# ScalarE evacuates the transposes before the exponential in every attention slot of a hybrid decoder layer

## The chip, the cores and the metric

The kernel runs on 1 core of one Trainium2 chip. The metric is device time in microseconds (us). An execution of the kernel before was also profiled: it took 1846.08 us, of which the program's instructions span 1844.3 us. The engines are called PE (TensorE), DVE (VectorE), ACT (ScalarE), POOL (GpSimd) and SP (SyncE).

## The reference

One decoder layer for 1024 tokens of width 1024. A normalised input is projected and mixed by three kinds of attention, whose outputs are gated per channel and projected; a grouped mixture of experts follows. Only the attention is touched here. Each query tile n (128 tokens, 8 tiles) does, cut to what matters:

```python
# NSA, 8 heads of 64, one KV head: compressed keys, selected blocks, window of 512
p_cmp = masked_softmax(q @ k_cmp, ...);  o_cmp = p_cmp @ v_cmp
_, sel = lax.top_k(block_scores(p_cmp), 8)
p = masked_softmax(q @ k_slc[sel], ...);  o_slc = p @ v_slc
p = masked_softmax(q @ k_win[last 512 + own tile], ...);  o_win = p @ v_win
# stick breaking, 4 heads: z = q @ k;  a = exp(z + running sum of -softplus(z));  o = a @ v
# sliding window of 128 with sinks, 4 heads
p = exp(s - max);  o = (p @ v) / (sum(p) + exp(sink - max))
```

A merge gate, `sigmoid(h @ w_in[merge columns])`, weights the three branches. Its matrix products do not depend on the attention.

## The kernel before

The attention is written as a list of slots. A query tile n from 0 to 7 has 20 slots, i from 0 to 19: `win` heads 0 to 7 at i = 0 to 7, then `slc` heads with a `swa` (sliding window) head at i = 9, 12, 15 and 18. Slot q = 20 n + i. Every slot has one unit (kind, head, n), with scores over `nb` blocks of 128 keys: n + 1 for `slc`, at most 5 for `win`, 2 for `swa` (1 at n = 0). A stick-breaking head (`sb`, n + 1 blocks) rides along in slots i = 6, 9, 12, 15.

In slot q, **PE** does in this order: the scores of unit q; the transposes of the units in `s["T"]`; the products with the values of units transposed earlier; the scores of the ride; and a third of a merge-gate product (8 matmuls of 512 columns; slots 2 to 147, but for two slots). `s["T"]` holds first the unit of slot q - 1. In 55 of 160 slots it holds a second one:

- i = 3: the compressed probabilities (`cmp`, 4 blocks)
- i = 4: the token outputs of tile n - 1 (`out`, 8 blocks; not at n = 0)
- i = 5: the selection mask (`sel`, 1 block)
- i = 10, 13, 16, 19: the `sb` unit of slot q - 4

Where there are two, the gate product is issued between the transposes of the first and those of the second (`if j == 1: gate_matmuls(q)`, L1985 to L1987). The values of the first unit follow the second's transposes, except with `sel` and `out`, where they come before them and nothing follows.

Transposes are written to PSUM in groups of up to 4 blocks. Groups have a running number g over all slots; even ones are evacuated by **ACT** (L396), odd ones by **DVE** (L398), both in `evacuate_groups`, which waits for `t_full` of each group. From the planner's numbering, the second unit has an even group in these slots: every `sb` (i = 10, 13, 16, 19 at every n), every `out`, `cmp` only for n of 4 and more, `sel` only for n below 4.

**DVE** in slot q: the row maximum of the scores of unit q (L1393, for `swa` L1389 and L1391, gives `max_ok`), its groups, softmax sums and other small work.

**ACT** in slot q, strictly in program order: waits for `max_ok`, does the exponential of unit q (L981, gives `p_ok`; for `swa` a small one of the sinks before it, L979); its groups of `s["T"]`; parts of the stick-breaking chain (L991, L992 at i = 7, 10, 13, 16, L998 at i = 9, 12, 15, 18); the copy of the ride's scores (L1004); the copy of a finished gate product out of PSUM (L1013), after which SP sends it to DRAM and loads the gate weights of the product after next; and rounding of newly landed gate weights (L956, in `gate_weights_hi`), which waits for their DMA.

Who waits for the exponential of unit q: its own transposes in slot q + 1 (L1903), and scores that reuse its banks (`wait_scores_read`). Scores of more than 4 blocks need banks 0 and 1 together, so for n of 4 and more the scores of a `win` or `slc` unit in slot q + 1 wait for the exponential of the `win` or `slc` unit in slot q. `swa` scores use bank 2.

Of the kernel before, what the change touches and what calls it, by code (L numbers as in the profile page):

```python
# [59 lines left out]
def hybrid_trunk(nc, x, c, w_ada, b_ada, g_norm_mix, g_norm_moe, w_in, cmp_pe_k, cmp_w1_k, cmp_w2_k, cmp_pe_v,  # L60
                 cmp_w1_v, cmp_w2_v, nsa_q_gain, nsa_k_gain, swa_q_gain, swa_k_gain, swa_sinks, w_branch_a,
                 w_branch_b, w_branch_c, w_out, w_router, router_bias, w_exp_gate, w_exp_up, w_exp_down, out):
    _, T, D = x.shape
    NT, NK = T // P, D // P
    NE, DE = w_exp_gate.shape[1], w_exp_gate.shape[3]
# [18 lines left out]
    with ctx:  # L84
# [132 lines left out]
        def slot_of(i):  # L217
            return HOME[i]
# [3 lines left out]
        for i in ORDER:  # L222
            s = slot_of(i)
# [123 lines left out]
        def ride(q, d):  # L347

            r = slots[q - d]["ride"] if q >= d else None
            return (r, width(r), r["n"] * SB_H + r["h"]) if r else (None, 0, 0)  # L350

        def score_buf(u):
            return psum[:, u["banks"][0]:u["banks"][-1] + 1, :].rearrange("p a b -> p (a b)")
# [17 lines left out]
        def width(u):  # L371
            return (u["n"] + 1 - u["lo"]) * P

        def group(u, j):

            return psum[:, 4 + u["groups"][j] % 2, :], range(4 * j, min(4 * j + 4, u["nb"]))

        def evacuate_groups(eng, u, parity):

            for j, g in enumerate(u["groups"]):  # L380
                if g % 2 != parity:
                    continue
                bank, blocks = group(u, j)
                w = len(blocks) * P
                eng.wait_ge(t_full, g + 1)
                if u["kind"] == "sel":
                    src = bank[ROW_SEL:AUG, 0:P].unsqueeze(1).to_broadcast([NSEL, NSA_H, P])
                    dst = qaT[ROW_SEL:AUG, u["n"], :, :]
                elif u["kind"] == "out":
                    src, dst = bank, heads[:, (u["n"] * 2 + j) * BANK:(u["n"] * 2 + j + 1) * BANK]  # L390
                else:
                    if u["v"] >= 2:
                        eng.wait_ge(pv_done, u["v"] - 1)
                    src, dst = bank[:, 0:w], probT[u["v"] % 2][:, 4 * j * P:4 * j * P + w]
                if parity == 0:
                    ins = nc.scalar.activation(dst, src, ACT.Copy)  # L396
                else:
                    ins = nc.vector.tensor_copy(dst, src)  # L398
                ins.then_inc(t_free[parity], 1)
# [29 lines left out]
        def gate_steps(q):  # L429

            d, mid = q - FILL0, 3 * N_GATE // 2
            if mid <= d < mid + SPLIT_SLOTS:
                return 0, None
            if d >= mid:
                d -= SPLIT_SLOTS
            g, c = divmod(d, 3)
            return (g, c) if 0 <= g < N_GATE else (0, None)
# [410 lines left out]
        def _(act):  # L848
# [87 lines left out]
            def out_hi(n):  # L936
                if n == 0:
                    act.wait_ge(g_full, N_GATE)
                for g in out_of[n]["groups"]:
                    wait_evacuated(act, g)  # L940
                act.activation(o_hi[:, n, :, :], o_raw[:, n, :, :], ACT.Copy).then_inc(o_hi_ok, 1)

            def tokens_hi(hf):
                act.wait_ge(gab_out, 16)
                for kh in range(2):
                    ks = slice(4 * kh, 4 * kh + 4)
                    if hf == 0:
                        act.wait_ge(acc_full, 4 * NT + 8)
                    else:
                        act.wait_ge(g_full, N_GATE // 2)  # L950
                    act.activation(hT_hi[hf][:, ks, :], hT_half[hf][:, ks, :], ACT.Copy).then_inc(h_hi_ok, 1)

            def gate_weights_hi(i):
                u, kh = divmod(i, 2)
                act.wait_ge(gate_in[u % 2], 16 * (u // 2 + 1))
                act.activation(gate_hi[kh], gate_piece(i, 0), ACT.Copy).then_inc(gw_hi_ok, 1)  # L956
# [5 lines left out]
            def branch_weights_hi(m):  # L962
                act.wait_ge(branch_in[m % 2], 16 * 3 * (m // 2 + 1))
                if m >= 2:
                    act.wait_ge(mix_full, 6 * (m - 1))
                act.activation(branch_hi(m), branch_w(m), ACT.Copy).then_inc(bw_hi_ok, 1)

            for q, s in enumerate(slots):
                u = s["unit"]
                if u:  # L970
                    k, w = u["kind"], width(u)
                    act.wait_ge(max_ok, q + 1)
                    if q >= 2:
                        act.wait_ge(t_full, slots[q - 2]["unit"]["groups"][-1] + 1)
                    src = score_buf(u)[:, 0:w]
                    col = {"win": 0, "slc": NSA_H, "swa": 2 * NSA_H}[k] + u["h"]
                    if k == "swa":
                        src = swa_s[u["h"] % 2][:, 0:w]
                        act.activation(sink_e[:, u["h"]:u["h"] + 1], sink[:, u["h"]:u["h"] + 1], ACT.Exp,  # L979
                                       bias=negm[:, q % 4:q % 4 + 1])  # L980
                    act.activation(prob[q % 2][:, 0:w], src, ACT.Exp, bias=negm[:, q % 4:q % 4 + 1],  # L981
                                   accum_out=den[:, u["n"] % 2, col:col + 1]).then_inc(p_ok, 1)
                for t in s["T"]:
                    evacuate_groups(act, t, 0)
                if "cmp" in s:
                    act.wait_ge(cmp_in, s["n"] + 1)
                    act.activation(cmp_p, cmp_s, ACT.Exp).then_inc(cmp_e, 1)
                r, w, m = ride(q, 1)
                if r:
                    act.wait_ge(sb_zc, m + 1)  # L990
                    own(act.activation(zc[:, 0:w], zc[:, 0:w], ACT.Exp))  # L991
                    act.activation(zc[:, 0:w], zc[:, 0:w], ACT.Ln, bias=1.0).then_inc(sb_ln, 1)  # L992
                r, w, m = ride(q, 3)
                if r:
                    act.wait_ge(sb_arg, m + 1)
                    if m:
                        act.wait_ge(t_full, rides[m - 1]["groups"][-1] + 1)
                    act.activation(prob_b[:, 0:w], zs[:, 0:w], ACT.Exp).then_inc(pb_ok, 1)  # L998
                r, w, m = ride(q, 0)
                if r:  # L1000
                    act.wait_ge(s_full, r["s"] + 1)
                    if m:
                        act.wait_ge(pb_ok, m)
                    act.activation(zs[:, 0:w], score_buf(r)[:, 0:w], ACT.Copy).then_inc(sb_z, 1)  # L1004
                g, c = gate_steps(q)
                if c == 0 and g + 1 < N_GATE:
                    act.wait_ge(gate_first, g + 1)
                    gate_weights_hi(2 * g + 2)
                if c == 2:
                    act.wait_ge(g_full, g + 1)  # L1010
                    if g >= 2:
                        act.wait_ge(z_out[g % 2], 16 * (g // 2))
                    act.activation(z_stage[g % 2], GATE_BANK, ACT.Copy).then_inc(z_ok, 1)  # L1013
                    if g + 1 == N_GATE // 2:
                        tokens_hi(1)
                    if g + 1 < N_GATE:
                        gate_weights_hi(2 * g + 3)
                if 0 <= q - SPLIT0 < NT - 1:
                    out_hi(q - SPLIT0)
                elif 0 <= q - SPLIT0 - (NT - 1) < 2:  # L1020
                    branch_weights_hi(q - SPLIT0 - (NT - 1))
# [1167 lines left out]
```

## Time and profile before

| what | value |
|---|---|
| median of 3 runs | 1845.61 us (1844.99 to 1848.99) |
| profiled execution | 1846.08 us, span 1844.3 us |
| PE busy | 1729.1 us, 94% of the span |
| DVE busy | 1008.0 us, 55% |
| ACT busy | 723.2 us, 39% |
| POOL busy | 367.8 us, 20% |
| attention slots | from 325 to 1150 us of the span |

Shares are over the whole span. The attention slots lie between the projection and compression ahead of them and the mixing, output projection and experts behind them. In timelines of single slots, the start and duration of an instruction show what it waited for and what waited for it.

### The profile page before, as it was taken

The numbers are of one execution on the slowest core, as the hardware profiler recorded it, in microseconds if no ns is written. First come the engines' busy times: TensorE is split into PE (matmuls) and PEld (weight loads), VectorE is DVE, ScalarE is ACT, GpSimd is POOL, SyncE is SP. The second block draws the span as 40 slices with busy tenths as digits, with TensorE's granted clock in tenths as the row PEclk, the third lists the DMA queues.
The fourth block names the chain that finished last, engine by engine and source line by source line (L and its number), as shares of the span: only waits on it lengthen the run. The fifth ranks groups of instructions, "written<-read, shape, count | busy, mean of one in ns | idle before, by whom it ended". The sixth has DMA issues, their size and how long they took to land. (4 is left out here: it accounts for less than half of the span.)

```text
span 1844.3 us, 23578 instructions
## 1 busy us (share of the span) xinstructions
PE 1729.1 (94%) x8557; PEld 1316.0 (71%) x8557; DVE 1008.0 (55%) x1643; ACT 723.2 (39%) x1251; POOL 367.8 (20%) x316
## 2 busy tenths in 40 slices
PE   6999999799999899999999988999948999999996
PEld 5555554677777686877867766878846888888885
DVE  5654322554555555544544556676565656567485
ACT  1421110444354444444444355332132545446373
POOL 4211140001010101002011021000003253436355
PEclk9999999899999899999999998999978999999998
DMA  9434321132122111111111110654264787879694
GB/s 352 167 137 160 92 69 25 57 86 69 52 69 58 46 48 39 53 51 36 52 35 41 35 52 11 243 200 186 92 226 139 252 270 267 273 267 332 216 370 133
DMA packets 146665, 247.13 MB, mean 134 GB/s; under 512 B 6264, under 2 KB 69824, under 8 KB 145248
## 3 DMA queue, kind: packets, MB, share of 16 engines
q1 hardware_dynamic: 138384, 217.28, 34.6%
q0 software_dynamic: 7984, 27.93, 6.2%
q8 instruction: 64, 1.05, 0.2%
q10 hardware_dynamic: 192, 0.54, 0.1%
q14 instruction: 41, 0.34, 0.1%
HBM read 210.60 MB, written 36.18 MB: 134 GB/s over the span
## 5 line engine op out<-in xcount | busy, mean ns | idle before, releaser
L773 POOL TENSOR_SCALAR arena<-arena 128x128 f32<-128x128 f32 (+7 forms) x32 | 77.4, 2418 | 728.2 <-ACT arena L1004 728.2
L1945 PE MATMUL psum<-kv,arena 128*128 128x64 f32 x1464 | 190.4, 273 | 7.5 <-DVE arena L1340 6.5
L1945 PEld LDWEIGHTS psum<-kv,arena 128*128 128x128 f32 x1464 | 185.1, 197 | 11.1 <-issue 7.0
L1785 PE MATMUL psum<-arena 128*128 128x512 f32 (+2 forms) x512 | 188.1, 521 | 0.3 <-DVE arena L1163 0.3
L1393 DVE TENSOR_REDUCE negm<-psum 128x1 f32<-128x640 f32 (+7 forms) x128 | 90.4, 706 | 173.4 <-PE psum L1886 171.6
L981 ACT ACTIVATE arena<-psum,negm 128x640 f32<-128x640 f32 (+7 forms) x128 | 89.5, 699 | 180.1 <-DVE negm L1393 179.8
L1884 PE MATMUL psum<-kv,heads 112*128 112x512 f32 (+7 forms) x384 | 149.7, 495 | 6.9 <-ACT arena L1004 6.4
L2122 PE MATMUL psum<-heads_r,kv_r 128*128 128x512 f32 x384 | 150.4, 392 | 3.2 <-DVE kv_r L1655 3.2
L1649 DVE TENSOR_TENSOR arena_r<-arena,heads_r 128x2048 fp32r<-128x2048 f32 x64 | 142.5, 2287 | 15.1 <-ACT heads_r L1074 15.1
L1785 PEld LDWEIGHTS psum<-arena 128*128 128x128 f32 x512 | 95.6, 191 | 76.7 <-issue 73.2
L1913 PE MATMUL psum<-ident,arena 128*128 128x128 f32 x828 | 131.7, 283 | 19.8 <-ACT arena L981 16.2
L2123 PE MATMUL psum<-heads_r,kv_r 128*128 128x512 f32 x384 | 150.1, 391 | 0.0
L1913 PEld LDWEIGHTS psum<-ident,arena 128*128 128x128 f32 x828 | 94.5, 145 | 55.6 <-issue 23.6
L820 POOL TENSOR_TENSOR arena_r<-arena,bc_r 128x2048 fp32r<-128x2048 f32 x16 | 102.8, 6423 | 105.4 <-ACT bc_r L1074 105.4
L1074 ACT ACTIVATE heads_r<-arena 128x2048 fp32r<-128x2048 f32 x64 | 117.3, 1915 | 7.2 <-DMA out_dram<-heads 4.3
L1884 PEld LDWEIGHTS psum<-kv,heads 112*128 112x128 f32 (+1 forms) x384 | 68.7, 199 | 41.6 <-issue 27.8
L2127 PE MATMUL psum<-arena_r,kv_r 128*128 128x512 f32 x384 | 95.0, 389 | 0.0
L398 DVE COPY arena<-psum 128x512 f32<-128x512 f32 (+3 forms) x140 | 67.9, 485 | 47.7 <-PE psum L1913 47.4
L956 ACT ACTIVATE arena_r<-arena 128x512 fp32r<-128x512 f32 x96 | 59.9, 625 | 84.5 <-DMA arena<-in_w_in_dram 76.9
L396 ACT ACTIVATE arena<-psum 128x512 f32<-128x512 f32 (+3 forms) x140 | 66.5, 475 | 52.4 <-PE psum L1913 52.4
L2122 PEld LDWEIGHTS psum<-heads_r,kv_r 128*128 128x128 f32 x384 | 72.6, 189 | 18.7 <-issue 3.6
L2123 PEld LDWEIGHTS psum<-heads_r,kv_r 128*128 128x128 f32 x384 | 72.6, 189 | 15.1
(421 smaller groups left out, 3381.9 us busy)
## 6 DMA issues: line engine op xcount, KB each, us to landing
arena<-in_w_exp_gate_dram SPq DMA_DIRECT2D x16, 2048.0 KB, 11.6
arena<-in_w_exp_down_dram SPq DMA_DIRECT2D x16, 2048.0 KB, 12.3
arena<-in_w_exp_up_dram SPq DMA_DIRECT2D x16, 2048.0 KB, 13.4
arena<-in_w_in_dram SPq DMA_DIRECT2D x48, 512.0 KB, 4.1
arena<-in_w_ada_dram SPq DMA_DIRECT2D x7, 2048.0 KB, 8.7
z_dram<-arena SPq DMA_DIRECT2D x48, 256.0 KB, 2.3
arena<-z_dram SPq DMA_DIRECT2D x8, 1536.0 KB, 7.3
bc<-in_w_ada_dram SPq DMA_DIRECT2D x4, 2048.0 KB, 7.8
```

The source lines that it names most:

```text
L820: pool.tensor_tensor(ew_lo(e, 2)[:, SLOT // 2:SLOT], w_raw(e, 2)[:, SLOT // 2:SLOT], ew_hi[2][:, SLOT // 2:SLOT].bitcast(F32), ALU.subtrac ...
L981: act.activation(prob[q % 2][:, 0:w], src, ACT.Exp, bias=negm[:, q % 4:q % 4 + 1], accum_out=den[:, u["n"] % 2, col:col + 1]).then_inc(p_o ...
L1074: act.activation(ew_hi[i][:, cs], w_raw(e, i)[:, cs], ACT.Copy).then_inc(w_hi_ok, 1)
L1393: dve.tensor_reduce(m1, score_buf(u)[:, 0:w], AX.X, ALU.max, negate=True).then_inc(max_ok, 1)
L1649: dve.tensor_tensor(ew_lo(e, i)[:, cs], w_raw(e, i)[:, cs], ew_hi[i][:, cs].bitcast(F32), ALU.subtract).then_inc(w_lo_ok, 1)
L1785: mm = pe.matmul(psum[:, 4 + s % 3, 0:w], hT[:, k, n * P:(n + 1) * P], slot(slot_of(L_TOK + ch))[:, k, 0:w], start=(k == 0), stop=(k == NK ...
L1884: mm = pe.matmul(b[:, c0:c1], lhs, keys[:, k0 + c0:k0 + c1], start=True, stop=not masks)
L1913: ins = pe.transpose(bank[:, c * P:(c + 1) * P], src[:, t * P:(t + 1) * P], ident[:, :])
L1945: mm = pe.matmul(psum[:, bank, c * HD:(c + 1) * HD], pt[:, j * P:(j + 1) * P], v, start=(j == 0), stop=(j == u["nb"] - 1))
L2122: pe.matmul(out, xs_hi[:, k, :], w_hi[:, k, :], start=(k == 0), stop=False)
L2123: pe.matmul(out, xs_lo[:, k, :], w_hi[:, k, :], start=False, stop=False)
L2127: mm = pe.matmul(out, xs_hi[:, k, :], w_lo[:, k, :], start=False, stop=(k == NK - 1))
```

## The change

ACT's loop over `s["T"]` is moved ahead of the exponential. The order of PE, DVE, POOL and SP is not edited, nor is any operation added, removed or resized.

```diff
             for q, s in enumerate(slots):
                 u = s["unit"]
+                for t in s["T"]:
+                    evacuate_groups(act, t, 0)
                 if u:
                     k, w = u["kind"], width(u)
                     act.wait_ge(max_ok, q + 1)
...
                     act.activation(prob[q % 2][:, 0:w], src, ACT.Exp, bias=negm[:, q % 4:q % 4 + 1],
                                    accum_out=den[:, u["n"] % 2, col:col + 1]).then_inc(p_ok, 1)
-                for t in s["T"]:
-                    evacuate_groups(act, t, 0)
                 if "cmp" in s:
```

## Rows read from the trace of the kernel before

**Rows 1.** Busy time in the attention slots: PE, weight loads, DVE, ACT, POOL; granted clock
```profile
325.00:1150.00 825.00, 777.75 (x4388) 604.60 (x4388) 427.99 (x821) 369.56 (x798) 78.36 (x39) 0.95 0.18 49
```

**Rows 2.** Waits in the attention slots: total us, times, longest us
```profile
PE psum L1913 <- ACT arena L981: 16.2, 8, 6.8
...
PE psum L1945 <- DVE arena L1340: 6.5, 5, 1.8
PE psum L1884 <- ACT arena L1004: 6.4, 3, 2.4
```

**Rows 3.** Timeline, slot 93 (n = 4, i = 13): start us, duration us, instruction
```profile
738.14 0.80 ACT L981 ACTIVATE arena<-psum,negm 128x640 f32<-128x640 f32 x1 [3.19 <-DVE negm L1393]
...
738.83 0.20 ACT L981 ACTIVATION_READ_ACCUMULATOR arena<-psum,negm 128x1 f32 x1
...
740.91 0.60 ACT L396 ACTIVATE arena<-psum 128x512 f32<-128x512 f32 x1 [1.88 <-PE psum L1913]
...
741.21 1.08 PE L1884 MATMUL psum<-kv,heads 112*128 112x512 f32 x2
741.40 0.73 ACT L991 ACTIVATE arena<-arena 128x640 f32<-128x640 f32 x1
```

**Rows 4.** Timeline, slot 156 (n = 7, i = 16)
```profile
1123.16 1.11 ACT L981 ACTIVATE arena<-psum,negm 128x1024 f32<-128x1024 f32 x1 [3.10 <-DVE negm L1393]
...
1127.34 0.60 ACT L396 ACTIVATE arena<-psum 128x512 f32<-128x512 f32 x1 [2.70 <-PE psum L1913]
...
1127.56 0.65 PE L1884 MATMUL psum<-kv,heads 112*128 112x512 f32 x1
```

**Rows 5.** Timeline, end of slot 84 (n = 4, i = 4, second unit `out`)
```profile
687.21 1.02 PE L1884 MATMUL psum<-kv,heads 65*128 65x512 f32 x2
687.41 0.60 ACT L396 ACTIVATE heads<-psum 128x512 f32<-128x512 f32 x1 [3.30 <-PE psum L1913]
```

**Rows 6.** Timeline, end of slot 83 (n = 4, i = 3, second unit `cmp`)
```profile
679.82 0.60 ACT L396 ACTIVATE arena<-psum 128x512 f32<-128x512 f32 x1 [1.45 <-PE psum L1913]
...
680.68 1.08 PE L1884 MATMUL psum<-kv,heads 65*128 65x512 f32 x2
```

**Rows 7.** Timeline, slot 45 (n = 2, i = 5, second unit `sel`)
```profile
500.95 0.58 ACT L981 ACTIVATE arena<-psum,negm 128x384 f32<-128x384 f32 x1 [0.24 <-DVE negm L1393]
...
503.21 1.02 ACT L396 ACTIVATE heads<-psum 16x1024 f32<-16x1024 f32 x1 [1.59 <-PE psum L1911]
...
503.72 0.50 PE L1913 MATMUL psum<-ident,arena 128*128 128x128 f32 x3
```

**Rows 8.** Timeline, end of slot 53 (n = 2, i = 13, second unit `sb`)
```profile
535.04 0.49 ACT L396 ACTIVATE arena<-psum 128x384 f32<-128x384 f32 x1 [1.80 <-PE psum L1913]
...
536.00 0.49 PE L1913 MATMUL psum<-ident,arena 128*128 128x128 f32 x3
```

**Rows 9.** Timeline, tile 0: PE at slot 7, then slot 9
```profile
355.86 0.33 PE L1913 MATMUL psum<-ident,arena 128*128 128x128 f32 x1 [1.07 <-ACT arena L981]
...
364.24 0.63 ACT L956 ACTIVATE arena_r<-arena 128x512 fp32r<-128x512 f32 x1 [4.47 <-DMA arena<-in_w_in_dram]
...
365.34 0.25 ACT L396 ACTIVATE arena<-psum 128x128 f32<-128x128 f32 x1
...
365.49 0.33 PE L1913 MATMUL psum<-ident,arena 128*128 128x128 f32 x1 [0.77 <-ACT arena L981]
```

**Rows 10.** Timeline, tile 7: PE waits behind an evacuation by ACT
```profile
1074.86 0.41 PE L1913 MATMUL psum<-ident,arena 128*128 128x128 f32 x2 [0.89 <-ACT arena L396]
...
1119.17 0.70 PE L1884 MATMUL psum<-kv,heads 112*128 112x512 f32 x1 [2.39 <-ACT arena L1004]
```

**Rows 11.** A PE wait of slot 110, and busy time with granted clock behind it and in slot 117
```profile
838.77 0.63 PE L1945 MATMUL psum<-kv,arena 128*128 128x64 f32 x4 [1.70 <-DVE arena L1340]
...
840.50:847.30 6.80, 6.80 (x28) 6.07 (x26) 4.18 (x4) 1.27 (x3) 0.00 (x0) 0.50 0.00 0
877.10:882.50 5.40, 5.40 (x34) 4.15 (x33) 4.64 (x6) 3.08 (x6) 0.00 (x0) 1.00 0.02 3
```

## The prediction

> **What bounds the kernel now.** I read the windows of the attention slots first. PE is busy 777.8 of 825 us there, DVE 428 and ACT 370 [rows 1]. So a microsecond that PE is made to wait for ACT is a microsecond of the span, and time saved on ACT alone is worth nothing. Next the list of waits: what PE waits for from ACT is small, 16.2 us for the exponential in front of its own transposes, 6.4 us for the copy of the ride's scores (L1004) [rows 2]. Then the timelines of single slots, to see who is first ready in each. In slot 93 ACT had been idle 3.19 us when the exponential's maximum came; the exponential started at 738.14, in the middle of PE's slot. The second unit's even group was ready only at 740.91, after the gate product, and PE began the next scores at 741.21 [rows 3]. The reader is to see the order of these three: the exponential long done, the group at the end of the slot, the next scores 0.3 us behind it.
>
> **The change, part by part.** Nothing is added or removed: the same evacuations and exponentials run, in the other order. DMAs are not moved on SP; they shift only as far as ACT's copies do.
>
> *Slots with one unit to transpose (104).* The first unit's groups are full about when the maximum comes, while ACT sits idle (3.19 us in slot 93, 3.10 in slot 156 [rows 3, 4]), and the exponential is needed only in the next slot, after values and a gate product. I cost this at nothing; the cover is the gate product, and where it is missing see the gains below.
>
> *Slots with two units, n of 4 and more.* ACT now waits for the second unit's even group before it does the exponential. Queued behind that wait are the exponential, and behind it the stick-breaking pair L991 and L992 and the copies; on PE the next scores wait for the exponential, because both use banks 0 and 1. Slot 93: the evacuation starts at 740.91; the next instruction of ACT starts 0.49 us later, as L991 does at 741.40 now. The exponential with its accumulator read takes 0.89 (738.14 to 739.03), and PE starts 0.05 behind it: 741.40 + 0.89 + 0.05 = 742.34, where it started at 741.21 [rows 3]. That is 1.13 us of PE idle. The same working for i = 13 and 16 of the four tiles gives 0.9 to 1.5, the largest in slot 156: 1127.34 + 0.49 + 1.20 + 0.05 = 1129.08 against 1127.56, with an exponential over 1024 columns of 1.11 plus 0.09 [rows 4]. Sum of the eight: 9.3. At i = 10 PE waits for DVE's L1340 behind the second unit anyway [rows 2, 11], and the exponential is over by then: 0. At i = 19 the next tile's compressed scores cover it: 0, but for the last slot of all: 0.9. Together 10.2.
>
> *`out`, i = 4.* No values follow the second unit, so nothing covers. Slot 84: 687.41 + 0.49 + 0.89 + 0.05 = 688.84 against 687.21 [rows 5], 1.6; times four tiles 6.5. For n = 1 to 3 the next slot's scores use another bank and cover part: 0.6 to 0.7 each, 2.0. Together 8.5.
>
> *`cmp`, i = 3.* Ten value matmuls cover most: 679.82 + 0.49 + 0.89 + 0.05 = 681.25 against 680.68 [rows 6], 0.57; times four 2.2. For n below 4 the group is odd, DVE's: 0.
>
> *`sel`, i = 5, n below 4.* The evacuation is the long one, 1.02 us. Slot 45: 503.21 + 0.93 + 0.67 + 0.05 = 504.86 against 503.72 [rows 7], 1.1; slot 65 1.0. In slots 5 and 25 PE later waits for an exponential that is itself held by a gate weight DMA, 1.07 us in tile 0 [rows 9], and so I count only 0.25 and 0.5 of their 1.3. Together 2.9.
>
> *`sb`, n below 4.* Slot 53: 535.04 + 0.39 + 0.67 + 0.05 = 536.15 against 536.00 [rows 7, 8], 0.15. Nine such slots 1.3. In tile 0 about 0.37 in three, by way of the gate weights' round trip: 1.1. Together 2.4.
>
> *Slots where ACT came late.* In tiles 0 and 1 ACT is held by a gate weight DMA, and PE waits for the exponential directly behind it [rows 9]. There a ready evacuation now goes first, 0.25 to 0.38 us. Seven such slots, 1.9.
>
> Sum of losses: 10.2 + 8.5 + 2.2 + 2.9 + 2.4 + 1.9 = 28.1 us.
>
> *Gains.* In tile 7 the gate products are over, and PE waits directly for ACT: 0.89 us for an evacuation behind an exponential, 2.39 us for L1004 [rows 10]. In slots 149, 152 and 155 the group was full well before the maximum, so L1004 comes 0.5 earlier: 1.5. Transposes of slots 149, 152, 155 that waited for a bank gain 0.5, 0.3 and 0.4. Two waits for values in tiles 1 and 2 gain 0.7. Together 3.4. Losses less gains: 24.7.
>
> **The clock.** Behind a PE wait of 1.70 us the granted clock was 0.50 (1.2 GHz) from 840.5 to 847.3 [rows 11]. What 6.8 us do at that level, 3.4 do at the full 2.4 GHz: 3.4 us lost at most. By the matmuls, 28 there at 0.243 us each against 34 in the 5.4 us of slot 117 at 0.159, it is 28 × 0.084 = 2.4. I take 3.0 us a fall, between the two. Of the five waits of this kind, up to 1.8 us long [rows 2], I find a fall behind one. The change makes four new waits of 1.6 and eight of about 1.1; it shortens two waits of 2.5 (one is in [rows 10]) that have a fall behind them now. Between no new fall and six, less the two, I take one: 3.0.
>
> Forecast: 24.7 + 3.0 = 27.7 us on the profiled 1846.1, 1873.8, rounded to 1874. The median of the runs is 0.5 below the profiled execution, which I leave inside the rounding.
>
> **Rivals.**
>
> 1. *Faster: PSUM comes free sooner, and that decides.* PE waits for banks and for L1004 in tile 7 [rows 10]. If the late exponential were hidden everywhere (PE having 1.6 us of other work between a second unit's transposes and the next use of the exponential), the gains of 3.4 would stand alone, and the two falls behind L1004 might go, 2 times 3.0: up to 9.4, 1837 to 1843. Against it: the next scores start before that group is even evacuated, 687.21 against 687.41 [rows 5]. The Trainium skill, page PSUM — Partial Sum Buffer, section Summary: rules for kernel authors, says to evacuate PSUM promptly because it is small; by that alone this change would be this rival. Chance 0.03.
> 2. *No change: everything lost is taken back at waits of PE that are there anyway,* as in slots 5 and 25. PE's remaining waits are 47 us in all [rows 1], but the ones behind the lossy slots hang on PE's own progress (DVE's L1340 follows PE's transposes), so they move with it. Within 0.2%: 1842 to 1849. Chance 0.03.
> 3. *Half absorbed.* The short tiles, where DMA and ACT set the pace, give back all they lose (`sel`, `sb` below n = 4, late ACT: 2.9 + 2.4 + 1.9 = 7.2), and the two falls in tile 7 go (6.0): 24.7 - 7.2 - 6.0 = 11.5, 1858. Chance of 1849 to 1860: 0.12.
> 4. *The clock makes it worse.* Half of the twelve longest new waits have a fall behind them: 24.7 + 6 × 3.0 = 42.7, 1889; with all twelve 60.7, 1907. Chance of over 1888: 0.12.
>
> The forecast itself, 1860 to 1888, has 0.70.
>
> **How the numbers follow.** The range takes in rival 3's 1858 and rival 4's 1889; below and above I leave about one in ten each: 1856 to 1891. 0.2% is 3.7 us, about what a measurement of this kernel can tell from no change. Faster 0.03, same 0.03, slower 0.12 + 0.70 + 0.12 = 0.94.
>
> **What would show it.** In the profile after: ACT's evacuation at the end of slots i = 13, 16 and 4 followed by L981, and PE's L1884 there waiting for ACT L981 at twelve places more, 1.1 to 1.6 us each; L981's wait for DVE's maximum much shorter in total, and in its place waits of L396 for PE's transposes; PE's busy time in the attention slots about the same at a span some 28 us longer. L1004's three waits in tile 7 at about 1.9. The time outside 325 to 1150 us should not move. I would be wrong if PE reached the next scores only after the exponential even so, if the clock fell behind every new wait, or if falls that are there now went with the shifted times.

## The result: 1.8% slower

| | median | runs | profiled execution, span | mean granted clock |
|---|---|---|---|---|
| before | 1845.3 us | 4 (1839.79 to 1848.99) | 1846.08, 1844.3 | 0.962 |
| changed | 1876.36 us | 4 (1873.86 to 1877.49) | 1877.49, 1875.7 | 0.962 |

The ratio is 1.0176, 95% interval 1.0152 to 1.0199: 28 to 37 us slower. Forecast were 1874 us and a range of 1856 to 1891.

The attention slots start with the compressed scores of tile 0 and end with the first mixing product. Timeline of the kernel before, those two instructions (start us, duration us):

```profile
325.32 0.59 PE L1859 MATMUL psum<-stair,identb 128*128 128x512 bf16 x1 [0.84 <-DVE kcmpT L1298]
...
1150.77 0.76 PE L2018 MATMUL psum<-arena_r 128*128 128x512 f32 x1 [0.94 <-issue]
```

And of the changed one:

```profile
326.40 0.38 PE L1859 MATMUL psum<-stair,identb 128*128 128x512 bf16 x1 [0.84 <-DVE kcmpT L1298]
...
1181.02 0.77 PE L2018 MATMUL psum<-arena_r 128*128 128x512 f32 x1 [0.94 <-issue]
```

From one to the other it is 825.5 us before and 854.6 after: 29.2 of the 31.4 us of the two spans lie there. The remaining 2.2 lie in stages whose code is the same, where the forecast had nothing move.

Windows of the changed kernel over the attention slots (PE, weight loads, DVE, ACT, POOL busy; granted clock), which answers to [rows 1]:

```profile
325.00:1181.00 856.00, 783.27 (x4389) 605.55 (x4390) 430.56 (x824) 368.30 (x799) 78.38 (x39) 0.95 0.17 47
```

ACT and DVE do the same work. PE is idle 73 us instead of 47, and its recorded busy time for the same instructions is 5.5 us longer: at a new wait the start moves by about 0.16 us more than the idle time shown (slot 93: 1.13 against 0.96; slot 84: 1.63 against 1.46). What PE waits for is in the list of PE's waits of the changed kernel, which answers to [rows 2] (total us, times, longest us; L983 is the exponential, L981 before):

```profile
PE psum L1884 <- ACT arena L983: 25.4, 20, 2.6
PE psum L1913 <- ACT arena L983: 24.9, 19, 7.3
PE psum L1945 <- DVE arena L1340: 7.1, 5, 1.8
PE psum L1884 <- ACT arena L1004: 5.5, 3, 1.9
PE psum L1859 <- ACT arena L983: 2.8, 4, 1.0
```

And the one line of before that [rows 2] do not have:

```profile
PE psum L1884 <- ACT arena L981: 9.9, 4, 2.6
```

Scores that wait for the exponential went from 4 times to 20 and from 9.9 us to 25.4; transposes from 8 times to 19 and from 16.2 to 24.9. The sixteen new waits of the scores are those of slots i = 3, 4, 13 and 16 of tiles 4 to 7; the eleven of the transposes lie in two-unit slots of tiles 0 to 3, behind a late ACT, and in tile 7.

Slot 93 in the changed kernel's timeline, which answers to [rows 3]:

```profile
756.92 0.60 ACT L396 ACTIVATE arena<-psum 128x512 f32<-128x512 f32 x1 [5.96 <-PE psum L1913]
...
757.41 0.79 ACT L983 ACTIVATE arena<-psum,negm 128x640 f32<-128x640 f32 x1
...
758.09 0.20 ACT L983 ACTIVATION_READ_ACCUMULATOR arena<-psum,negm 128x1 f32 x1
758.18 0.73 ACT L991 ACTIVATE arena<-arena 128x640 f32<-128x640 f32 x1
758.35 0.30 PEld L1884 LDWEIGHTS psum<-kv,heads 112*128 112x128 f32 x2 [1.10 <-ACT arena L983]
758.35 1.35 PE L1884 MATMUL psum<-kv,heads 112*128 112x512 f32 x4 [0.96 <-ACT arena L983]
```

ACT stood idle for 5.96 us, waiting for transposes; the maximum had been ready since 754.1. Evacuation to exponential is 0.49 us, exponential with its read 0.88, PE 0.06 behind. PE's scores start 1.43 us after the evacuation's start, where it was 0.30 before: 1.13 later, the number of the forecast. Slot 84, which answers to [rows 5]:

```profile
701.70 0.60 ACT L396 ACTIVATE heads<-psum 128x512 f32<-128x512 f32 x1 [4.40 <-PE psum L1913]
702.20 0.79 ACT L983 ACTIVATE arena<-psum,negm 128x640 f32<-128x640 f32 x1
...
703.13 1.13 PE L1884 MATMUL psum<-kv,heads 65*128 65x512 f32 x2 [1.46 <-ACT arena L983]
```

Scores 1.43 behind the evacuation's start, where they were 0.20 ahead of it: 1.63.

### The profile page after: what moved, and what is told of

It is laid out like the page before. It is cut to its first block and busy times, and to the rows that moved or that the text cites. A ratio compares the mean times of both kernels' runs of the same rounds, so it can differ in the third digit from the quotient of the medians.

```text
span 1875.7 us, 23578 instructions
## 1 busy us (share of the span) xinstructions
PE 1736.4 (93%) x8557; PEld 1317.9 (70%) x8557; DVE 1009.2 (54%) x1643; ACT 721.7 (38%) x1251; POOL 367.8 (20%) x316
## 5 line engine op out<-in xcount | busy, mean ns | idle before, releaser
L396 ACT ACTIVATE arena<-psum 128x512 f32<-128x512 f32 (+3 forms) x140 | 67.4, 482 | 239.3 <-PE psum L1913 238.8
L1913 PE MATMUL psum<-ident,arena 128*128 128x128 f32 x828 | 133.0, 285 | 27.0 <-ACT arena L983 24.9
L1649 DVE TENSOR_TENSOR arena_r<-arena,heads_r 128x2048 fp32r<-128x2048 f32 x64 | 142.4, 2286 | 15.1 <-ACT heads_r L1074 15.1
L983 ACT ACTIVATE arena<-psum,negm 128x640 f32<-128x640 f32 (+7 forms) x128 | 89.0, 695 | 32.6 <-DVE negm L1393 32.3
```

The costliest lines, as they stand in the source:

```text
L1649: dve.tensor_tensor(ew_lo(e, i)[:, cs], w_raw(e, i)[:, cs], ew_hi[i][:, cs].bitcast(F32), ALU.subtract).then_inc(w_lo_ok, 1)
L1913: ins = pe.transpose(bank[:, c * P:(c + 1) * P], src[:, t * P:(t + 1) * P], ident[:, :])
```

## The experiments

Twelve experiments, ten of them edited kernels. Each ratio is to runs of the kernel before on the same chip, which experiments made together share, with a 95% interval; microseconds are worked out from the ratio on 1845.

**1. Which of the evacuations costs?** Only the first unit's goes ahead of the exponential:

```diff
-                for t in s["T"]:
+                for t in s["T"][:1]:
                     evacuate_groups(act, t, 0)
...
+                for t in s["T"][1:]:
+                    evacuate_groups(act, t, 0)
                 if "cmp" in s:
```

> ACT evacuates only the first unit's even groups ahead of the exponential; those of the second unit stay behind it. Theory (the loss is the wait for the second unit's group): what is left is the late ACT of tiles 0 and 1, +1.9 us, and the gains of 3.4 us: 1.5 us faster than before, 0.9992, and no new PE wait for the exponential at i = 3, 4, 13, 16. Rival (any evacuation ahead of the exponential delays it and costs): most of the +31 us stays, at least +15.

Measured: 1836.43 us against 1844.94, ratio 0.9953 (0.9939 to 0.9967), 9 us faster. The whole loss is gone, so it belongs to the second unit's evacuation; the rival is out. The gain is larger than the 1.5 expected; the table behind run 12 shows that most of it goes with the clock. PE's waits in this kernel (line numbers of its edit shift by two):

```profile
PE psum L1915 <- ACT arena L983: 16.2, 10, 6.8
PE psum L1886 <- ACT arena L983: 9.9, 4, 2.6
PE psum L1947 <- DVE arena L1342: 6.7, 5, 1.8
PE psum L1886 <- ACT arena L1006: 5.5, 3, 1.9
```

Scores wait 4 times again, 9.9 us, as before; and waits for the scores' copy keep the changed kernel's 5.5.

**2 and 3. Do the kinds of second units add up?** In one run `cmp`, `out` and `sel` stay behind the exponential, in the other `sb`:

```diff
+                late = [t for t in s["T"][1:] if t["kind"] != "sb"]   # run 3: == "sb"
+                for t in s["T"][:len(s["T"]) - len(late)]:
+                    evacuate_groups(act, t, 0)
...
+                for t in late:
+                    evacuate_groups(act, t, 0)
                 if "cmp" in s:
```

> As the change, but cmp, out and sel are evacuated behind the exponential; sb stays ahead. Theory: 10.2 + 2.4 (sb) + 1.9 (late ACT) - 3.4 (gains) = +11.1 us on the kernel before. Rival (the clock or an alignment makes the loss): all or nothing, within 3 us of before or of the change (+31).

Measured: ratio 1.0081 (1.0052 to 1.0110), +15 us. Its seven runs fall in two groups, three at 1849.7 to 1853.2 us with a mean granted clock of 0.965 and four at 1863.3 to 1868.2 with 0.957 to 0.960, so the +15 lies between two values.

> The complement: sb is evacuated behind the exponential, cmp, out and sel ahead. Theory: 8.5 + 2.2 + 2.9 + 1.9 - 3.4 = +12.1 us. Together with the sb run, less the common -1.5, it should give the whole change. Rival as there.

Measured: ratio 1.0085 (1.0061 to 1.0109), +16 us. Both kinds cost, about alike, each 3 to 4 us over the expectation but with it inside the interval. The two minus what they share (run 1, -9) make +39, where the change has +32. The intervals are 3 to 5 us to either side, so the split is shown to be about even, not more.

**4 and 5. Is the exponential of these slots on PE's path?** It is done twice in 12 slots, in the changed kernel (run 4) and in the kernel before (run 5):

```diff
+                    if s["n"] >= 4 and s["i"] in (4, 13, 16):
+                        own(act.activation(prob[q % 2][:, 0:w], src, ACT.Exp, bias=negm[:, q % 4:q % 4 + 1]))
                     act.activation(prob[q % 2][:, 0:w], src, ACT.Exp, bias=negm[:, q % 4:q % 4 + 1],
                                    accum_out=den[...]).then_inc(p_ok, 1)
```

> The change, with the exponential done twice (the first result is overwritten) in the 12 slots of n = 4 to 7, i = 4, 13, 16. Theory (the exponential of these slots is on PE's path): each costs its own duration once more, 4 x 0.85 + 2 x (0.85 + 0.95 + 1.05 + 1.15) = 11.4 us on top of the change, so +42 on the kernel before. Rival (ACT has slack there, the loss comes from somewhere else): nothing on top, +31.

Measured: 1901.39 us, ratio 1.0306 (1.0284 to 1.0329). That is 24 us more than the change costs, double the 11.4 expected. PE's waits in this kernel:

```profile
PE psum L1886 <- ACT arena L985: 35.9, 20, 2.6
PE psum L1915 <- ACT arena L985: 24.1, 19, 7.3
```

Scores wait 35.9 instead of 25.4 us: 10.5 more, near the 11.4 of the arithmetic. The rest fits what the clock took. Span and mean granted clock of this kernel, and of the changed one:

```profile
core 0: 1903.2 us, clock 0.951
```

```profile
core 0: 1875.7 us, clock 0.962
```

Time at the lower level counts half, so span times (1 - clock) is what the clock took away at most: 71 us in the change, 93 here in the slowest of four runs and 89 as their mean. In the change the twelve waits are recorded with 0.75 to 1.46 us and cost next to no clock in sum; with 1.3 to 2.5 us, 0.9 more on average, the same twelve do.

> The kernel before, with the exponential done twice in the same 12 slots. Theory: there it ends 1 to 3 us ahead of PE's need, but in slot 153, where 0.6 us are left: +0.7 us. Rival (work added on ACT costs wherever it stands): +11.4 us.

Measured: ratio 1.0020 (1.0000 to 1.0041), 0 to 8 us, with 0.7 inside and 11.4 outside. The same work on ACT is nearly free before the change and costs in full after it. That shows the path.

**6 and 7. Does the place of the gate product decide?** It is issued last in every slot, with ACT's new order (run 6) and its old one (run 7):

```diff
                 for j, u in enumerate(s["T"]):
-                    if j == 1:
-                        gate_matmuls(q)
...
-                if len(s["T"]) < 2:
-                    gate_matmuls(q)
+                gate_matmuls(q)
```

> The change, with the gate product issued behind the last transposes and values of a slot in every slot, instead of between the two units. Theory: the gate product of over 2 us now lies between the second unit's transposes and the next scores and hides evacuation and exponential; lost are only the three slots of tile 7 without gate products, 1.1 + 1.5 + 0.9, and the late ACT, 1.9, less the gains of 3.4: +2 us on the same placement with ACT's old order. Rival (the order on ACT costs by itself): +25 to +31 us on it.

Measured: 1852.7 us, ratio 1.0032 (1.0019 to 1.0045).

> The partner: ACT's old order, gate product last. Theory: the second unit's transposes wait for the first's bank at few places, so 0 to +5 us on the kernel before. No rival differs here; it is the base of the run with the change.

Measured: 1867.67 us, ratio 1.0118 (1.0092 to 1.0145). The rival of run 6, a loss of 25 us or more on the same placement, is out: with the gate product last, ACT's new order is 16 us *faster* than its old one (1.0032 against 1.0118). My own numbers are out too, +2 for the pair and at most +5 for run 7. The lists of PE's waits say why. Old order, gate product last:

```profile
PE psum L1945 <- ACT arena L396: 16.9, 14, 2.6
PE psum L1913 <- ACT arena L981: 14.5, 7, 5.6
...
PE psum L1913 <- ACT arena L396: 7.3, 11, 1.1
```

New order, gate product last:

```profile
PE psum L1913 <- ACT arena L983: 17.4, 11, 5.6
PE psum L1945 <- DVE arena L1340: 11.4, 8, 2.4
PE psum L1945 <- DVE arena L398: 9.1, 10, 1.3
PE psum L1884 <- ACT arena L983: 6.9, 6, 1.4
```

Without the gate product between the units, values and the second unit's transposes come straight behind the first's. The values need the copy that ACT makes of the first unit's bank, the transposes need a bank that ACT has emptied, and ACT does both only after the exponential: 24.2 us in 25 waits. The new order leaves one of them, 0.5 us, and the exponential is then hidden by the gate product behind it: scores wait 6 times, 6.9 us, and four of these are the waits at i = 6 that the old order has too. Both orders with the gate product last are slower than the kernel before. I had looked only at what comes late in the new order, not at what comes late in the old one once its cover is moved.

**8. The gains alone.** First unit early from slot 148 on, everything else as before:

```diff
+                early = s["T"][:1] if q > SPLIT0 - 2 else []
+                for t in early:
+                    evacuate_groups(act, t, 0)
...
+                for t in s["T"][len(early):]:
+                    evacuate_groups(act, t, 0)
                 if "cmp" in s:
```

> First unit ahead of the exponential only from slot 148 on, where gate products are over; the rest is the kernel before. Theory: the gains alone, -2.7 us (three times 0.5 at L1004, and 0.5, 0.3, 0.4 at transposes), 0.9985. Rival (PE takes no profit, its waits for ACT there are only bookkeeping): 0.

Measured: 1835.28 us (1833.45 to 1837.12), ratio 0.9940 (0.9924 to 0.9957), 11 us faster. It is on a par with run 1, and these two are the fastest kernels of this study. Its span and clock, and those of before:

```profile
core 0: 1834.4 us, clock 0.967
```

```profile
core 0: 1844.3 us, clock 0.962
```

The clock took 60.5 us here and 70.1 before, so up to 9.6 of the 9.9 us between the two profiles are clock. Most of it lies in slots that were not edited. The compressed scores of tile 7, which come ahead of the first edited slot, start at 1018.26 us before and at 1010.31 here:

```profile
1018.26 0.38 PE L1859 MATMUL psum<-stair,identb 128*128 128x512 bf16 x1
```

```profile
1010.31 0.38 PE L1862 MATMUL psum<-stair,identb 128*128 128x512 bf16 x1
```

What the edit itself gave is therefore far less than 11 us.

**9 and 10. How far do the same kernels repeat?** Both once more, unedited.

> The kernel before once more, unedited. Theory (the length of the stretches at the lower clock depends on where the waits fall, not on the program alone): the waits agree with the first profile within 1 us, but the falls behind the four equal waits at i = 6 are not all of the same length as in the first profile; the time is within 3 us of before. Rival (falls belong to the program): the same falls at the same places.

Measured: ratio 0.9990 (0.9977 to 1.0003). The waits for the exponential agree (scores 9.9 us in 4, transposes 16.6 in 7); those at L1004 are 5.6 us instead of 6.4. The granted clock fell behind the wait of slot 126 (n = 6, i = 6) for 3.4 us instead of 6.8 by the two traces' clock records, and the tile behind it was 1.6 us shorter. So for the kernel before, the theory holds.

> The changed kernel once more, unedited, on the chip of these runs. Theory: +28 to +34 us, PE waiting for the exponential the same 50 us as in the first profile within 1 us, the falls elsewhere in part. Rival: the same falls.

Measured: ratio 1.0166 (1.0136 to 1.0195), +31 us. Waits again 25.4 and 24.5 us; but here the falls were the same 14 in the same places with the same lengths as in the first profile. For these two executions of the changed kernel the rival holds. It does not hold for all: a third one beside it took 1883.32 us at a clock of 0.957 against 0.962. What decides is open.

**11. A wait that the prediction left out.** The second unit of slot i = 19 of tiles 0 to 3 stays behind the exponential:

```diff
+                late = s["T"][1:] if s["i"] == 19 and s["n"] < 4 else []
```

> The change, but in slot i = 19 of tiles 0 to 3 the second unit's group stays behind the exponential. Theory (the next tile's compressed scores use the bank of slot 19's unit, and so wait for its exponential, which the prediction left out): PE's waits at the compressed scores' first matmul go from 6 us (matmul and load rows together) to under 1.5, 2.9 us less than the change in time. Rival (the shift at the tile boundary has another cause): those waits stay, no difference.

Measured: 1873.06 us against 1877.37 for run 10 beside it, ratio 1.0134 (1.0109 to 1.0158) against 1.0166. The direction is right and 2.9 is within the uncertainty of the 4.3 between the medians. The trace is clearer; in the changed kernel and here (L1862 is L1859 there):

```profile
PE psum L1859 <- ACT arena L983: 2.8, 4, 1.0
```

```profile
PE psum L1862 <- ACT arena L984: 0.3, 1, 0.3
```

**12. Can a shift alone do what run 8 did?**

```diff
+            for _ in range(8):
+                own(dve.tensor_copy(v_cmp[0:HD, 0:HD], psum[0:HD, 3, 0:HD]))
             own(dve.tensor_copy(v_cmp[0:HD, 0:HD], psum[0:HD, 3, 0:HD]))
```

> The kernel before, with one small copy of the key compression on DVE repeated eight times ahead of the first slot; the slots are unedited and start about 1.7 us later (8 x 0.205). It asks what an edit costs or gives through the clock alone, since the run that changes only slots from 148 on was 10 us faster, of which its waits explain about 3. Theory (falls of the clock have another place and length once the slots start later): the time is off +1.7 by 3 us or more, and the stretches at the lower clock add up to another sum. Rival (falls follow the waits of the program, wherever they start): +1.7 us, within 2.

Measured: 1845.08 us (1839.95 to 1851.62), ratio 1.0005 (0.9987 to 1.0022), +1 us. The time speaks for the rival, +1.7 us, though the interval reaches from -2 to +4. The profiled execution, at 1841.27, is one of the faster ones of this kernel; it has

```profile
core 0: 1839.5 us, clock 0.965
```

that is 64.4 us taken by the clock against 70.1. One such execution shows no effect of the shift: the unedited kernel beside it had clocks from 0.958 to 0.966.

**All executions, with the clock's part taken out.** A profile is one execution, but span and mean granted clock are on record for every execution. Span times (1 - clock) is the clock's part at most; the time less this is the rest. Over the 73 executions of the kernel before that stand beside the experiments, the time goes from 1836.35 to 1851.15 us with clocks from 0.967 to 0.958, and the rest is 1774.6 on average, with a standard deviation of 1.7. The differences below are of means, in us, to all executions of the kernel before on that chip; so the time column differs from the ratios by up to 2 us. A difference in the rest is uncertain by 1 to 2.5 us:

| run | time | clock's part | rest | expected |
|---|---|---|---|---|
| the change (run 10) | +30.7 | +1.3 | +29.4 | +24.7 and 3.0 of clock |
| 1, first unit only | -8.5 | -6.1 | -2.4 | -1.5 |
| 2, `sb` early | +15.1 | +2.5 | +12.6 | +11.1 |
| 3, the others early | +14.5 | +4.3 | +10.2 | +12.1 |
| 4, change, exponential twice | +57.1 | +19.3 | +37.8 | 11.4 on the change |
| 5, before, exponential twice | +3.1 | +2.2 | +0.9 | +0.7 |
| 6, change, gate last | +7.7 | -3.8 | +11.4 | +2 on run 7 |
| 7, before, gate last | +23.5 | -5.3 | +28.8 | 0 to +5 |
| 8, first unit from slot 148 | -9.7 | -8.5 | -1.2 | -2.7 |
| 11, change, slot 19 late | +25.4 | -2.2 | +27.5 | 2.9 less than the change |
| 12, before, shifted | +0.6 | -0.1 | +0.6 | +1.7 |

Where the expectation was worked out from waits alone, it is within 3 us of the rest in all but runs 6 and 7 and the change itself, 4.7 us off, of which 2.9 are a wait left out (run 11). By this bound the gains of runs 1 and 8 are for the most part the clock's, on average over their executions and not in one trace alone, and so is more than half of what run 4 adds to the change. The rests of runs 2 and 3 less that of run 1 make 25 of the change's 29.

## Why the prediction was right

**The loss in two-unit slots at n of 4 and more: right, term by term.** From the starts of the scores in the two traces, slots 84, 104, 124 and 144 got 1.68, 1.69, 1.68 and 1.69 us later (1.63 worked out), the four `cmp` slots 0.56 each (0.57), and the eight `sb` slots 0.9 to 1.6 (0.9 to 1.5). PE's recorded waits there are about 0.16 us shorter than these shifts. The order of events is that of the forecast. Runs 1, 4 and 5 confirm it by experiment, not only by the trace.

**Slots that were costed at nothing: right.** In run 1, where the first unit's evacuation is all that moves, nothing is lost, and PE's waits for the exponential are the same 16.2 and 9.9 us.

**Missed: the tile boundary of tiles 0 to 3.** The prediction took i = 19 as covered by the next tile's compressed scores. For n below 4, those scores use bank 2 and so does the unit of slot 19; they themselves wait for its exponential. The four starts of those scores got 2.9 us later in all; the waits are 2.8 us, where the kernel before has 0.4, and 0.3 without the cause (run 11).

**Mis-sized: the clock.** I added 3.0 us for one more fall. The mean granted clock is 0.962 in both, so over the whole span the clock took 70.1 us before and 71.3 after, and over all executions on one chip 1.3 us more (run 10). In the attention slots alone the stretches at the lower level add up to 81.3 us before and 82.4 after, by the two traces' clock records: 0.5 us. The new waits do bring falls. Behind the one of slot 104:

```profile
820.73 0.70 PE L1884 MATMUL psum<-kv,heads 65*128 65x512 f32 x1 [1.46 <-ACT arena L983]
```

```profile
822.30:825.30 3.00, 3.00 (x11) 2.52 (x10) 1.50 (x2) 1.05 (x3) 0.00 (x0) 0.50 0.03 5
```

But others became shorter: behind slot 110's wait, still 1.70 us, the stretch is 3.4 us instead of 6.8. That the two cancel is not something the forecast had worked out. The two errors, 2.9 missed and 2.5 too many, have opposite signs, and the forecast is nearer than its parts by luck: 24.7 + 2.9 + 0.5 = 28.1 against 29.2 in the attention slots.

**The gains: the direct part smaller than forecast, and the rest not foreseen.** Waits at L1004 went from 6.4 to 5.5 us: two of the three got 0.48 shorter, where 0.5 was forecast for each of three. The sum alone would not show it, since the unedited kernel of run 9 has 5.6. Those for an evacuation in front of transposes, 1.3 us, are gone from the list, but half of that comes back at the next wait for DVE's L1340, 1.48 us instead of 0.83. Forecast was 3.4 in all. Kernels with the gains and no losses (runs 1 and 8) are 9 and 11 us faster, the 9.4 of the faster rival, which I had given 0.03 because the losses would outweigh it; they did. Without the clock's part they are 2.4 and 1.2 us faster. That rival had 6.0 of its 9.4 us from two falls behind L1004 in tile 7, but in run 8's clock record both are still there, 3.4 and 6.8 us long as before, so its number was met in another way than it said. Where the clock's part comes from stays open: run 12 did not bring it about by a shift, and in run 8 the clock differs from before in slots with the same code.

**The rivals.** "No change" and "half absorbed" are out by the interval: 28 to 37 us. What they got right is slots 5 and 25, where PE's later wait took part of the loss back: in slot 5, 1.2 of 1.5 us. "The clock makes it worse" is not this change, but it is run 4, with waits 0.9 us longer. The Trainium skill, page PSUM — Partial Sum Buffer, section Summary: rules for kernel authors, says to evacuate promptly. Run 1 agrees with it for groups that are already full when ACT gets to them, by the 2.4 us left without the clock's part; run 8's 1.2 is within its uncertainty. The change, and run 3 against run 1, show the other side: a promptly placed evacuation of a group that is not yet full delays what is queued behind it.

## What to carry to other kernels

In an in-order engine's program, placing a step early is placing its wait early: ask not only whether the step is urgent but when its input is ready, and what behind it is needed first. Hoist what is ready, here the first unit (0.9953, of which 2.4 us are left without the clock's part), and leave behind what is filled at the end of the stage (1.0176 with both). The same hoist can turn its sign with the order on another engine: with the gate product last it was 16 us faster than the old order, though both were slower than the kernel before, so the two orders have to be costed together, each against its own waits.

## What the runs showed of the hardware

- Short PE waits are priced unevenly. Twelve added waits of 0.75 to 1.46 us left the mean granted clock at 0.962; lengthened by about 0.9 us each they took it to 0.951 to 0.954, and the time grew by 24 us for 10.5 us of longer waits.
- The clock can fall behind a short wait: it was 0.50 from 822.3 to 825.3 us behind a wait of 1.46 us.
- The clock's falls differ between executions of one kernel while its waits for the exponential agree, and move single executions by several us around the median (1836.35 to 1851.15 over 73 of the kernel before). A difference of a few us between two traces can be that alone. With 12 runs against 20, the 0.5% of run 1 has an interval of 0.14% to either side. Taking out span times (1 - clock) leaves a standard deviation of 1.7 us.
- An ACT instruction starts about 0.1 us before the one ahead of it is recorded as ended: L396 takes 0.60 and the next begins 0.49 behind its start. Adding recorded durations of evacuation, exponential and read end to end would have overstated the loss by about 0.2 us in each of the twelve slots, by this estimate some 2 us.
